# An encoder trunk on one core: the SSD scan rebuilt from log-decay tiles, loops written out, one convolution tap moved to ScalarE

## The chip, the cores and the metric

One core of a Trainium2 chip runs the whole program. The metric is the device time of one execution in microseconds (us), lower is better. TensorE (PE) multiplies matrices into eight PSUM banks, VectorE (DVE) and ScalarE (ACT) work elementwise, GpSimd (POOL) makes constants and issues some DMAs, SyncE (SP) issues the weight loads. Semaphores written by hand order the engines.

## What is computed

Two requests of 256 tokens (512 together) pass two layers of: half-step SwiGLU, a mixing stage, half-step SwiGLU. The mixing stage adds a convolution branch and a two-way state-space scan (SSD), each behind a gate. The scan, cut to what matters (one direction; `q` is a chunk of 128 tokens, so a request has two chunks):

```
    a = dtc * A ;  a_cum = jnp.cumsum(a, axis=2) ;  xdt = xc * dtc[..., None]
    seg = a_cum[:, :, :, None] - a_cum[:, :, None, :]
    decay = jnp.exp(jnp.where(tril, seg, -jnp.inf))
    scores = jnp.einsum("bcign,bcjgn->bcijg", Cc, Bc)
    y_diag = jnp.einsum("bcijgr,bcjgrp->bcigrp", scores[..., None] * decay, xdt)
    states = jnp.einsum("bcjgn,bcjgrp->bcgrpn", Bc, xdt * exp(a_cum[:, :, -1:] - a_cum))
    ... states carried from chunk to chunk ...
    y_off = jnp.einsum("bcign,bcgrpn->bcigrp", Cc, prev) * jnp.exp(a_cum)[..., None]
    y = y_fwd + y_bwd + xs * D_skip
```

x, B and C come out of a 5-tap convolution over tokens and a SiLU; the convolution branch has 31 taps.

## The kernel before

All activations stand as tiles of 128 features by 512 tokens. A **slab** is a 128x1024 block of weights: SP loads it into one of four slots (`wraw`), ACT rounds it to `whi` (L445), DVE makes the remainder `wlo` (L765), and PE multiplies eight pieces of it, three matmuls of 512 columns each (24 in all, L1139). ACT and DVE split a slab three slabs ahead of PE.

The mixing stage of a layer goes over eight groups of four heads, and two rounds more for gates. A group is eight steps `t` = 0 to 7, and in each step every engine does its share in program order: PE multiplies one slab (the projections gate, a, B, C, x, x, z, z of group `g`) and puts a piece of the SSD of group `g-1` behind it; DVE does four steps of the 5-tap convolution of `g`, some of the 31 taps of group `g-1` (`unit_tap`, L928, cut over the steps by `TAP_SLICES`), and its part of the SSD. So each layer has eight SSD groups, 16 in the program.

The SSD of a group, before, on PE: at t=0 transposes of x (L1297) and of B (L1303), and the scores of each chunk (L1307, 128x128 fp32); at t=1 the norm's sum (L1313) and, at t=1 and t=2, `seg` for four chunks in two directions: a product with `rtm` (L1249), the mask `never` (L1251) and four narrow products, one for each head (L1254); at t=3 the states (L1330), at t=4 their use for the other chunk (L1337); at t=4 and t=5 the product of weights and x with 64 moving columns for each chunk and head (`y_chunks`, L1264), and at t=5 and t=6 the transposes of that result (L1274). ACT takes the exponentials (`exp_seg`, L593), copies x, B, scores and states out of PSUM. DVE adds the two directions and multiplies by the scores (`decays`, L956, L961), scales x (L999), adds the states' part (L1014, L980), and gates. GpSimd sends the gated branch `tg` to DRAM (`v_spill`) and back into a padded tile (`vp`). Ahead of group 0, `dt_steps` makes the step sizes and sums of log decays, and DVE zeroes the pads (L1060, L1061).

Layers, groups 2 to 7 of a layer, and the feed-forward parts are hardware loops (`Fori`), with register arithmetic for semaphore values and addresses.

Of the kernel before, what the change touches and what calls it, by code (L numbers as in the profile page):

```python
# [5 lines left out]
F32 = mybir.dt.float32  # L28
F32R = mybir.dt.float32r
# [13 lines left out]
def trunk(nc, io):  # L43
# [47 lines left out]
    ND, NA = 16, 6  # L91
    NB = NC // 2

    v_dram = nc.dram_tensor("v_spill", [2, KD, P, SEQ], F32, kind="Internal").ap()
# [8 lines left out]
    with ExitStack() as ctx:  # L103
# [10 lines left out]
        selr = sb("selr", [P, 2, 2 * NH])  # L114
# [29 lines left out]
        with ExitStack() as s2:  # L144
            wd_raw = sb("wd_raw", [P, 8, P], at=s2)
            wd_hi = sb("wd_hi", [P, 8, P], F32R, at=s2)
            wd_lo = sb("wd_lo", [P, 8, P], F32R, at=s2)
            dx = sb("dx", [2 * NH, T], at=s2)
            de = sb("de", [2 * NH, T], at=s2)
            du = sb("du", [2 * NH, T], at=s2)  # L150
            dl = sb("dl", [2 * NH, T], at=s2)
            dc = sb("dc", [2 * NH, T], at=s2)
            dtf = sb("dtf", [2 * NH, 2, T], at=s2)
            aT = sb("aT", [P, NC, 2 * NH], at=s2)
            cumS = sb("cumS", [P, NC, 2 * NH], at=s2)
            ddS = sb("ddS", [P, NC, 2 * NH], at=s2)
        mix = sb("mix", [P, KD, T])
        with ExitStack() as s3:
            E = sb("E", [P, NC, 2, HPG * P], at=s3)
        ga = sb("ga", [P, KD, T])  # L160

        with ExitStack() as s3:
            tg = sb("tg", [P, T], at=s3)
            xpad = sb("xpad", [P, 2, 2, SEQ + TAPS - 1], at=s3)
# [3 lines left out]
            SC = sb("SC", [P, NC, P], at=s3)  # L168
            bT = sb("bT", [P, NC, P], at=s3)
            ytm = sb("ytm", [P, 2, GF], at=s3)  # L170
            dtT = sb("dtT", [P, NC, 2 * NH], at=s3)
            exT = sb("exT", [P, NC, 2 * NH], at=s3)
            wT = sb("wT", [P, NC, 2 * NH], at=s3)
# [5 lines left out]
        with ExitStack() as s3:  # L179
            yz = sb("yz", [P, 2, T], at=s3)  # L180
            rg = sb("rg", [P, T], at=s3)
        mtmp = sb("mtmp", [P, 2, T])
        mu = sb("mu", [P, T])
        with ExitStack() as s3:
            xw = sb("xw", [P, NC, GF], at=s3)
            zcur = sb("zcur", [P, 2, T], at=s3)
            yoff = sb("yoff", [P, NC, GF], at=s3)
            vp = sb("vp", [P, 2, SEQ + 2 * HALO], at=s3)
            cacc = sb("cacc", [P, 2, T], at=s3)
            rt = sb("rt", [P, NC, P], F32R, at=s3)  # L190
            rtm = sb("rtm", [P, NC, P], F32R, at=s3)
            exg = sb("exg", [P, NC, HPG], at=s3)
            wg = sb("wg", [P, NC, HPG], at=s3)
            selg = sb("selg", [P, 2, 2, HPG], F32R, at=s3)
            cwg = sb("cwg", [P, DWK], at=s3)
        with ExitStack() as s4:
# [23 lines left out]
        wd_in, wd_hi_ready, wd_lo_ready, dt_ps, dt_dve, dt_act, dtr_ps, dtr_ev, rt_ps, rt_hi, rtm_hi = (  # L220
            sem(n) for n in "wd_in wd_hi_ready wd_lo_ready dt_ps dt_dve dt_act dtr_ps dtr_ev rt_ps rt_hi rtm_hi".split())
        rt_ready, cum_ps, ex_ready, wT_ready = (
            sem(n) for n in "rt_ready cum_ps ex_ready wT_ready".split())
        tg_ready, v_ready, v_out, pad_zero, pad_ready, cv_ready = (
            sem(n) for n in "tg_ready v_ready v_out pad_zero pad_ready cv_ready".split())
        conv_tap, bc_ready, z_ready, zcopied, small_ready, xt_ps, bt_ps, sc_ps, xt_ready, bt_ready, sc_ready, xw_ready = (
            sem(n) for n in "conv_tap bc_ready z_ready zcopied small_ready xt_ps bt_ps sc_ps xt_ready bt_ready sc_ready xw_ready".split())
        st_ps, st_ready, yoff_ps, yoff_ready, seg_ps, e_ready, t_ready, m_ready, y_ps, y_ready, yt_ps, gate_mid, gated, xd_ready = (
            sem(n) for n in "st_ps st_ready yoff_ps yoff_ready seg_ps e_ready t_ready m_ready y_ps y_ready yt_ps gate_mid gated xd_ready".split())
        gsq, gsq_sum, gst_ps, gln, gr_ready, y2_ready, y_out = (  # L230
            sem(n) for n in "gsq gsq_sum gst_ps gln gr_ready y2_ready y_out".split())
        vp_in, cw_ready, unit_tap_done, unit_done, c_out = (
            sem(n) for n in "vp_in cw_ready unit_tap_done unit_done c_out".split())
# [12 lines left out]
        TAP_SLICES = [(0, 8), (8, 14), (14, 18), (18, 23), (23, 27), (27, 29), (29, DWK), (DWK, DWK)]  # L246
        f32 = lambda ap: ap.bitcast(F32)
        chunk = lambda c: slice(c * P, (c + 1) * P)

# [12 lines left out]
        def _(sp):  # L262
# [11 lines left out]
            def ffn(L, f, base):  # L274
                s = L * NSLAB + base
                for p0, n in PARTS:
                    with sp.Fori(0, n // 2) as i:
# [4 lines left out]
                    with sp.Fori(0, KD // 4) as i:  # L282
# [5 lines left out]
            def columns(L, base, w, col):  # L288

                with sp.Fori(0, KD // 4) as i:  # L290
# [4 lines left out]
            with sp.Fori(0, DEPTH) as L:  # L295
                ffn(L, 0, 0)
                with sp.Fori(0, NG) as g:
# [7 lines left out]
                with sp.Fori(0, KD // 2) as i:  # L305
# [18 lines left out]
        def _(pool):  # L324
            g_ = nc.gpsimd

            for free, n in ((lo_ready, RING), (slab_done, RING), (sq_added, 1), (ab_free, 2), (pad_ready, 2), (cv_ready, 2), (z_ready, 2),
                            (conv_tap, 1), (xt_ps, 1), (xw_ready, 1), (yoff_ps, 1), (yoff_ready, 1), (sc_ps, 1),
                            (seg_ps, 1), (e_ready, 1), (m_ready, 1), (y_ps, 1), (y_ready, 1), (gated, 1), (xd_ready, 1),
                            (gst_ps, 1), (y2_ready, 1), (unit_tap_done, 1), (unit_done, 1), (y_split, 4), (ya_mid, 2)):  # L330
# [4 lines left out]
            g_.memset(selr[:, :, :], 0.0).then_inc(const_made, 1)  # L335
# [8 lines left out]
            n = 3  # L344
            for sign in range(2):
                for half in range(2):
                    pool.wait_ge(const_fix, n)
                    pool.sem_inc(pool_passed, 1)
                    g_.affine_select(out=selr[:, sign, :], in_=selr[:, sign, :], compare_op=ALU.not_equal,
                                     fill=1.0 - 2 * sign, base=-half * 2 * NH, pattern=[[-1, 2 * NH]],  # L350
                                     channel_multiplier=1).then_inc(const_fix, 1)
                    n += 1
# [7 lines left out]
            def group(L, g, slabs, ssd, norm):  # L360

                G = L * NG + g
                H = G - 1
                if ssd:

                    pool.wait_ge(seg_ps, H * NC + 1)
                    pool.wait_ge(yoff_ready, H * NB + 1)
                    pool.wait_ge(xw_ready, H + 1)
                    pool.wait_ge(ex_ready, L + 1)
                    pool.wait_ge(wT_ready, L + 1)  # L370
                    pool.sem_inc(pool_passed, 1)
                    h0 = g * HPG - HPG
                    src = selr[:, :, :].rearrange("p s (d h) -> p s d h", d=2)[:, :, :, bass.ds(h0, HPG)]
                    g_.tensor_copy(selg[:, :, :, :], src).then_inc(small_ready, 1)

                    for c in range(2):
                        src = wT[:, c:NC:2, bass.ds(h0 + c * NH, HPG)]
                        g_.tensor_copy(wg[:, c:NC:2, :], src).then_inc(small_ready, 1)

                    src = exT[:, :, :].rearrange("p (b c) x -> p b (c x)", b=2)[:, :, NH:3 * NH]  # L380
                    src = src.rearrange("p b (c h) -> p b c h", c=2)[:, :, :, bass.ds(h0, HPG)]
                    g_.tensor_copy(exg[:, :, :].rearrange("p (b c) h -> p b c h", b=2), src).then_inc(small_ready, 1)

                    pool.wait_ge(v_out, G * 16 + 16)
                    pool.wait_ge(pad_zero, L * 2 + 2)
                    pool.wait_ge(unit_done, H + 1)
                    pool.sem_inc(pool_passed, 1)
                    pool.dma_start(vp[:, :, HALO:HALO + SEQ],
                                   v_dram[:, bass.ds(g - 1, 1)].rearrange("r o p t -> p (r o) t")).then_inc(vp_in, 16)
                if slabs:  # L390
                    pool.wait_ge(v_ready, G + 1)
                    pool.sem_inc(pool_passed, 1)
                    pool.dma_start(v_dram[:, bass.ds(g, 1)].rearrange("r o p t -> p (r o) t"),
                                   tg[:, :].rearrange("p (r t) -> p r t", r=2)).then_inc(v_out, 16)
                if norm:
                    pool.wait_ge(y2_ready, G * 2 - 1)
                    pool.sem_inc(pool_passed, 1)
                    pool.dma_start(y_dram[bass.ds(g * 2 - 4, 2)].rearrange("k p t -> p k t"),
                                   yz[:, :, :]).then_inc(y_out, 16)
                if ssd:  # L400
                    pool.wait_ge(unit_done, H + 2)
                    pool.sem_inc(pool_passed, 1)
                    pool.dma_start(c_dram[:, bass.ds(g - 1, 1)].rearrange("r o p t -> p (r o) t"),
                                   cacc[:, 0, :].rearrange("p (r t) -> p r t", r=2)).then_inc(c_out, 16)

            with pool.Fori(0, DEPTH) as L:
# [5 lines left out]
                group(L, 0, True, False, False)  # L412
# [1026 lines left out]
```

## Time and profile before

| what | value |
|---|---|
| time, median of 3 runs | 3090.6 us (3089.87 to 3091.07) |
| the profiled execution: time / span | 3091.98 / 3090.5 us |
| PE busy | 3014.7 us (98%) |
| DVE / ACT busy | 1909.0 (62%) / 1210.4 us (39%) |
| POOL busy | 88.8 us (3%) |

The span is what the profile covers. Matmuls are pipelined: the duration of one is its time in the pipeline, and the price of one is the distance from its start to the start of the next. A share of busy time is a mean over stages with different limits.

### The profile page before, as it was taken

The numbers are of one execution on the slowest core, as the hardware profiler recorded it, in microseconds if no ns is written. First come the engines' busy times: TensorE is split into PE (matmuls) and PEld (weight loads), VectorE is DVE, ScalarE is ACT, GpSimd is POOL, SyncE is SP. The second block draws the span as 40 slices with busy tenths as digits, with TensorE's granted clock in tenths as the row PEclk, the third lists the DMA queues.
The fourth block names the chain that finished last, engine by engine and source line by source line (L and its number), as shares of the span: only waits on it lengthen the run. The fifth ranks groups of instructions, "written<-read, shape, count | busy, mean of one in ns | idle before, by whom it ended". The sixth has DMA issues, their size and how long they took to land.

```text
span 3090.5 us, 41274 instructions
## 1 busy us (share of the span) xinstructions
PE 3014.7 (98%) x13916; PEld 2499.7 (81%) x13916; DVE 1909.0 (62%) x2503; ACT 1210.4 (39%) x1611; POOL 88.8 (3%) x186
## 2 busy tenths in 40 slices
PE   7999989999999999999999998999999999999998
PEld 5888868888887787888878887888888877878886
DVE  5444578999993555444544445799899735554444
ACT  4322344445543434222342224444554444252223
POOL 0000000000000000000000000000000010000000
PEclk9999999999999999999999999999999999999999
DMA  4333322323234433333333332332333353333332
GB/s 144 95 95 95 96 69 83 97 85 89 84 95 124 132 103 89 102 95 96 96 96 95 95 95 82 85 86 82 95 91 89 86 167 98 96 88 98 99 92 78
DMA packets 523803, 298.34 MB, mean 97 GB/s; under 512 B 10399, under 2 KB 514215, under 8 KB 523687
## 3 DMA queue, kind: packets, MB, share of 16 engines
q1 hardware_dynamic: 511888, 261.65, 29.6%
q0 software_dynamic: 10176, 34.63, 3.3%
q8 instruction: 68, 1.11, 0.1%
q10 hardware_dynamic: 1623, 0.55, 0.1%
q14 instruction: 48, 0.39, 0.0%
HBM read 277.92 MB, written 18.87 MB: 96 GB/s over the span
## 4 chain that ended last, share of the span: by engine, by line
PE 94%; DVE 2%; issue 1%; ACT 1%; DMA 1%; DVEq 0%; ACTq 0%; SPq 0%; POOLq 0%; POOL 0%
PE bank L1139 84%; PE bank L1264 2%; PE bank L1254 2%; PE bank L1249 1%; PE bank L1251 1%; PE bank L1337 1%; PE bank L1330 1%; DMA yraw<-y_spill 1%; PE bank L1307 0%; PE bank L1361 0%; PE bank L1297 0%; PE bank L1274 0%; PE bank L1313 0%; DVE bc L949 0%; DVE acc L776 0%
## 5 line engine op out<-in xcount | busy, mean ns | idle before, releaser
L1139 PE MATMUL bank<-uhi,whi 128*128 128x512 f32 x2944 | 1166.3, 396 | 29.6 <-DVE ulo L807 21.6
L1139 PE MATMUL bank<-uhi,wlo 128*128 128x512 f32 x2944 | 1150.6, 391 | 0.0
L1139 PE MATMUL bank<-ulo,whi 128*128 128x512 f32 x2944 | 1149.3, 390 | 0.0
L765 DVE TENSOR_TENSOR wlo<-wraw,whi 128x1024 fp32r<-128x1024 f32 x496 | 605.5, 1222 | 307.7 <-ACT whi L445 297.1
L445 ACT ACTIVATE whi<-wraw 128x1024 fp32r<-128x1024 f32 x496 | 521.1, 1053 | 433.2 <-PE bank L1139 433.0
L1139 PEld LDWEIGHTS bank<-uhi,whi 128*128 128x128 f32 x2944 | 555.4, 189 | 150.0 <-issue 28.4
L1139 PEld LDWEIGHTS bank<-uhi,wlo 128*128 128x128 f32 x2944 | 554.8, 188 | 118.0
L1139 PEld LDWEIGHTS bank<-ulo,whi 128*128 128x128 f32 x2944 | 555.6, 189 | 113.3 <-issue 1.4
L1139 PE MATMUL bank<-hhi,whi 128*128 128x512 f32 x960 | 377.1, 393 | 7.4 <-DVE hlo L1041 4.1
L1139 PE MATMUL bank<-hhi,wlo 128*128 128x512 f32 x960 | 374.2, 390 | 0.0
L1139 PE MATMUL bank<-hlo,whi 128*128 128x512 f32 x960 | 374.2, 390 | 0.0
L928 DVE SCALAR_TENSOR_TENSOR cacc<-vp,cwg,cacc 128x512 f32<-128x512 f32 x464 | 322.1, 743 | 0.0
L1139 PEld LDWEIGHTS bank<-hhi,whi 128*128 128x128 f32 x960 | 180.6, 188 | 49.5 <-DVE hlo L1041 6.3
L1139 PEld LDWEIGHTS bank<-hlo,whi 128*128 128x128 f32 x960 | 180.7, 188 | 38.1 <-issue 1.0
L1139 PEld LDWEIGHTS bank<-hhi,wlo 128*128 128x128 f32 x960 | 180.5, 188 | 37.8
L530 ACT ACTIVATE hhi<-fb 128x512 f32 x88 | 55.6, 632 | 395.2 <-DVE fb L835 395.2
L949 DVE SCALAR_TENSOR_TENSOR bc<-xpad,prm,bc 128x512 f32<-128x512 f32 x256 | 191.4, 747 | 17.6 <-DVE bc L946 3.7
L849 DVE SCALAR_TENSOR_TENSOR xf<-bank,xf 128x512 f32 x64 | 44.2, 691 | 197.4 <-PE bank L1139 197.4
L832 DVE TENSOR_TENSOR fb<-bank,rbc 128x512 f32<-128x512 f32 x88 | 60.8, 690 | 140.9 <-PE bank L1139 140.9
L527 ACT ACTIVATE fa<-fa 128x512 f32<-128x512 f32 x88 | 55.6, 632 | 234.1 <-DVE fa L829 234.1
L642 ACT ACTIVATE xpad<-bank 128x512 f32<-128x512 f32 x64 | 38.3, 598 | 256.1 <-DVE bc L949 151.6
L838 DVE TENSOR_TENSOR hlo<-fb,hhi 128x512 f32 x88 | 60.9, 692 | 82.2 <-ACT hhi L530 82.2
(199 smaller groups left out, 2144.8 us busy)
## 6 DMA issues: line engine op xcount, KB each, us to landing
wraw<-in_ffn_w_up SPq DMA_DIRECT2D x179, 512.0 KB, 3.7
wraw<-in_w_in SPq DMA_DIRECT2D x160, 512.0 KB, 3.8
wraw<-in_ffn_w_down SPq DMA_DIRECT2D x64, 512.0 KB, 3.7
wraw<-in_ssd_w_out SPq DMA_DIRECT2D x32, 512.0 KB, 3.8
wraw<-in_ffn_w_down SPq DMA_DIRECT2D x32, 384.0 KB, 3.3
y_spill<-yz POOLq DMA_DIRECT2D x16, 512.0 KB, 3.1
yraw<-y_spill POOLq DMA_DIRECT2D x32, 256.0 KB, 3.5
wraw<-in_conf_w_out SPq DMA_DIRECT2D x16, 512.0 KB, 4.3
```

What stands on the lines that cost most here:

```text
L445: a_.activation(whi[:, t % RING, :], wraw[:, t % RING, :], ACT.Copy).then_inc(hi_ready, 1)
L527: a_.activation(fa[:, j, :], fa[:, j, :], ACT.Silu).then_inc(silu_ready, 1)
L530: a_.activation(hhi[:, bass.ds(i * 2 + j, 1), :], fb[:, j:j + 1, :], ACT.Copy).then_inc(hhi_ready, 1)
L765: v_.tensor_tensor(wlo[:, t % RING, :], wraw[:, t % RING, :], f32(whi[:, t % RING, :]), ALU.subtract).then_inc(lo_ready, 1)
L832: v_.tensor_tensor(fb[:, j, :], bank[2 * j + 1][:, :], rbc[:, :], ALU.mult).then_inc(ab_free, 1)
L838: v_.tensor_tensor(hlo[:, m, :], fb[:, j:j + 1, :], f32(hhi[:, m, :]), ALU.subtract).then_inc(hlo_ready, 1)
L849: v_.scalar_tensor_tensor(out=xf[:, m, :], in0=bank[4 + q % 2][:, :].unsqueeze(1), scalar=0.5, in1=xf[:, m, :], op0=ALU.mult, op1=ALU.add) ...
L928: v_.scalar_tensor_tensor(out=dst, in0=src, scalar=cwg[:, k:k + 1], in1=dst, op0=ALU.mult, op1=ALU.add).then_inc(unit_tap_done, 1)
L949: ins = v_.scalar_tensor_tensor(out=dst, in0=src, scalar=w, in1=dst, op0=ALU.mult, op1=ALU.add)
L1139: ins = t_.matmul(out, a[:, slot, w], b[:, at + k, :], start=start and k == 0 and a is whi and b is hi, stop=stop and k == nk - 1 and a is ...
L1254: ins = t_.matmul(out[:, chunk(h)], selg[:, 0, d, h:h + 1].broadcast_to([P, P]), rt[:, c, :], start=False, stop=h == HPG - 1, skip_group_c ...
L1264: ins = t_.matmul(bank[4][:, f:f + HEAD], E[:, c, 0, chunk(h)], xT[:, c, h * HEAD:(h + 1) * HEAD], start=True, stop=True)
```

## The change

**SSD.** The log decay from token j to token i becomes one product: a tile `R` holds, for a head, the rows of the table `Q` of running sums that belong to it (ACT copies `Q` scaled by a column of the selector `selm`: eight copies for each request and group), and `Lr` (same chunk) or `LX` (other chunk) is the left side. PE adds the mask as before. Each request has, for each chunk, both directions on the diagonal and the one direction that reaches the other chunk. There are no states, no transposes of B and no transposes of y: the scores are made for all 256 tokens of a request, the 128x256 weights `M` of a chunk and head multiply x from the right, and y comes out with features on partitions, two heads in the two halves of a bank. **Loops** are all written out. **5-tap convolution:** ACT makes the middle tap with its bias from the bank, and DVE adds four. **Gated branch:** written by DVE straight into one of two padded tiles `vp`, without DRAM; the 31-tap result is put into the same tile, and the last sum comes at t=7 in place of t=6. The preparation of a layer sets constant parts of `Q`, `Lr` and `LX` to 1.

The core of the diff:

```diff
-                def seg(c):
-                    for d in range(2):
-                        t_.matmul(heads, rtm[:, c, :], selg[:, 1, d, :].unsqueeze(2).broadcast_to([P, HPG, P]), start=True, ...
-                        t_.matmul(heads, identr[:, :], never[:, d, :].unsqueeze(1).broadcast_to([P, HPG, P]), ...
-                        for h in range(HPG):
-                            ins = t_.matmul(out[:, chunk(h)], selg[:, 0, d, h:h + 1].broadcast_to([P, P]), rt[:, c, :], ...
+                def seg_diag(r):
+                    pe.wait_ge(rs_ready, H * 16 + r * 8 + 8)
+                    need(pe, m_added, H * 4 + r * 2)
+                    need(pe, e_ready, H * EPG + r * EPR)
+                    for c in range(2):
+                        for d in range(2):
+                            out = heads(2 + 4 * c + d)
+                            t_.matmul(out, Lr[:, d, 2 * r + c, :], R[:, d, c, :, :], start=True, stop=False)
+                            t_.matmul(out, identr[:, :], never[:, d, :].unsqueeze(1).broadcast_to([P, HPG, P]), ...
+                def seg_cross(r):
+                    for c in range(2):
+                        pe.wait_ge(e_ready, H * EPG + r * EPR + 2 * c + 1)
+                        t_.matmul(heads(2 + 4 * c), LX[:, 2 * r + c, :], R[:, c, 1 - c, :, :], start=True, stop=True).then_inc(seg_ps, 1)
+                def y_rows(r):
+                    pe.wait_ge(m_ready, H * 4 + r * 2 + 2)
+                    for j in range(2):
+                        for c in range(2):
+                            for half in range(2):
+                                h = 2 * j + half
+                                ins = t_.matmul(bank[4 + r][half * HEAD:(half + 1) * HEAD, j * SEQ:(j + 1) * SEQ],
+                                                xT[:, 2 * r + c, h * HEAD:(h + 1) * HEAD],
+                                                M[:, r, c, h, :, :].rearrange("p c i -> p (c i)"), start=c == 0, stop=c == 1)
...
+                def selected(r):
+                    need(act, seg_ps, H * EPG + r * EPR)
+                    for d in range(2):
+                        for h in range(HPG):
+                            head = (g - 1) * HPG + h
+                            a_.activation(R[:, d, :, h, :], f32(Q[:, d, 2 * r:2 * r + 2, :]), ACT.Copy,
+                                          scale=selm[:, head:head + 1]).then_inc(rs_ready, 1)
...
+                        a_.activation(bc[:, j, :], bank[t % 2][:, :], ACT.Identity, scale=prm[:, mid:mid + 1],
+                                      bias=prm[:, P_CB + col:P_CB + col + 1]).then_inc(mid_tap, 1)
...
+                def scored(r):
+                    dve.wait_ge(sc_ready, H * 2 + r + 1)
+                    for c in range(2):
+                        dve.wait_ge(m_added, H * 4 + r * 2 + c + 1)
+                        dve.wait_ge(e_ready, H * EPG + r * EPR + 5 + c)
+                        part = M[:, r, c, :, :, :].rearrange("p h c i -> p h (c i)")
+                        v_.tensor_tensor(part, part, SC[:, 2 * r + c, :].unsqueeze(1).broadcast_to([P, HPG, SEQ]), ALU.mult)...
...
+                v_.memset(f32(Q[2 * NH:P, :, :, :]), 1.0).then_inc(ones_set, 1)
+                v_.memset(f32(Lr[0:2 * NH, :, :, :]), 1.0).then_inc(ones_set, 1)
+                v_.memset(f32(LX[0:2 * NH, :, :]), 1.0).then_inc(ones_set, 1)
...
-            with dve.Fori(0, DEPTH) as L:
+            for L in range(DEPTH):
```

On PE, in one group of the loop, steps 2 to 4 of the SSD before (each `L1139` slab between them is left out; L1249, L1251 and L1254 are `seg`, L1330 and L1337 the states and their use, L1264 the product with x):

```order
L1249 MATMUL bank6<-selg,rtm 128x512
L1251 MATMUL bank6<-never,identr 128x512
L1254 MATMUL bank6<-rt,selg 128x128 x4
L1249 MATMUL bank7<-selg,rtm 128x512
L1251 MATMUL bank7<-never,identr 128x512
L1254 MATMUL bank7<-rt,selg 128x128 x4
...
L1330 MATMUL bank6<-xw,bT 128x256 x2
L1330 MATMUL bank7<-xw,bT 128x256 x2
...
L1337 MATMUL bank6<-xw,bc 128x256 x2
L1337 MATMUL bank7<-xw,bc 128x256 x2
L1264 MATMUL bank4<-xT,E 128x64 x4
```

On PE, the same steps now (L1193 is `seg_cross`, L1185 and L1186 `seg_diag` of the second request, L1202 `y_rows` of the first):

```order
L1193 MATMUL bank2<-R,LX 128x512
L1193 MATMUL bank6<-R,LX 128x512
...
L1185 MATMUL bank6<-R,Lr 128x512
L1186 MATMUL bank6<-never,identr 128x512
L1185 MATMUL bank7<-R,Lr 128x512
L1186 MATMUL bank7<-never,identr 128x512
...
L1193 MATMUL bank2<-R,LX 128x512
L1193 MATMUL bank6<-R,LX 128x512
L1202 MATMUL bank4<-M,xT 64x256 x8
```

The narrow products are gone, the states' two products too, and the product with x has 256 moving columns in place of 64 and fills 64 output partitions in place of 128.

On ACT, step 2 and the start of step 3 of a group now (L378 is the split of a slab, L605 the middle tap, L607 the copy for the other taps, L545 an exponential, L531 `selected` for the second request):

```order
L378 ACTIVATE whi<-wraw 128x1024
L605 ACTIVATE bc<-bank0,prm 128x512
L607 ACTIVATE xpad<-bank0 128x2x256
L545 ACTIVATE M<-bank2 128x4x128
L545 ACTIVATE M<-bank6 128x4x128
L531 ACTIVATE R<-Q,selm 128x2x128 x8
L378 ACTIVATE whi<-wraw 128x1024
L605 ACTIVATE bc<-bank1,prm 128x512
```

Before, that place had a split, the copy into `xpad`, four exponentials and a split; the middle tap and the eight copies into `R` are new, and PE's `seg_diag` of step 3 waits for the last of the eight.

## Rows read from the trace of the kernel before

**Rows 1.** The page: busy engines; the fetch of instructions (queue 8).

```profile
PE 3014.7 (98%) x13916; PEld 2499.7 (81%) x13916; DVE 1909.0 (62%) x2503; ACT 1210.4 (39%) x1611; POOL 88.8 (3%) x186
...
q8 instruction: 68, 1.11, 0.1%
```

**Rows 2.** Busy time by stretch: one mixing group (columns as printed).

```profile
core 0: us, PE busy (x) PEld busy (x) DVE busy (x) ACT busy (x) POOL busy (x), PEclk, DMA share, GB/s
690.86:752.75 61.89, 61.89 (x320) 52.56 (x320) 56.80 (x83) 29.81 (x45) 3.72 (x8) 1.00 0.30 89
```

**Rows 3.** The chain that ended last, one mixing group: start, length, what.

```profile
690.86 1.73 PE bank L1264 x16
692.59 5.54 PE bank L1139 x24
698.57 10.94 PE bank L1139 x48
711.71 5.47 PE bank L1139 x24
721.57 5.50 PE bank L1139 x24
730.59 5.53 PE bank L1139 x24
736.12 1.73 PE bank L1330 x8
737.85 5.47 PE bank L1139 x24
743.32 1.73 PE bank L1337 x8
```

**Rows 4.** PE in order of time, step 0 of that group: start, us, instruction.

```profile
709.34 1.03 PE L1297 MATMUL bank<-ident,bc 128*128 128x128 f32 x8
710.22 0.60 PE L1303 MATMUL bank<-ident,bc 128*128 128x128 f32 x4
710.65 1.06 PE L1307 MATMUL bank<-bc 128*128 128x128 f32 x8
711.47 0.47 PE L1139 MATMUL bank<-uhi,whi 128*128 128x512 f32 x1
```

**Rows 5.** PE in order of time, step 2 of that group.

```profile
726.91 0.38 PE L1249 MATMUL bank<-selg,rtm 128*128 128x512 f32 x1
727.12 0.40 PE L1251 MATMUL bank<-never,identr 128*128 128x512 f32 x1
727.36 0.56 PE L1254 MATMUL bank<-rt,selg 128*128 128x128 f32 x4
```

**Rows 6.** PE in order of time, group 0: a product with 64 output partitions.

```profile
432.05 1.94 PE L1229 MATMUL bank<-ul,aT 128*64 128x256 f32 x8
433.92 0.71 PE L1234 MATMUL bank<-aT,ul 128*128 128x128 f32 x4
```

**Rows 7.** PE's groups in that mixing group: busy, mean ns | idle.

```profile
L1330 PE MATMUL bank<-xw,bT 128*128 128x256 f32 x8 | 1.9, 379 | 0.0
```

**Rows 8.** DVE's groups in that mixing group.

```profile
L961 DVE TENSOR_TENSOR E<-E,SC 128x512 f32<-128x512 f32 x4 | 2.6, 684 | 0.0
L946 DVE TENSOR_SCALAR bc<-xpad,prm 128x512 f32<-128x512 f32 x4 | 2.2, 540 | 0.0
L999 DVE TENSOR_TENSOR xw<-xT,wg 128x1024 f32<-128x1024 f32 x1 | 1.2, 1219 | 0.0
L992 DVE SCALAR_TENSOR_TENSOR tg<-tg,bank 128x512 f32<-128x512 f32 x1 | 0.7, 687 | 2.3 <-PE bank L1139 2.3
```

**Rows 9.** ACT's groups in that mixing group.

```profile
L593 ACT ACTIVATE E<-bank 128x512 f32<-128x512 f32 x8 | 4.2, 596 | 1.8 <-PE bank L1254 1.8
L666 ACT ACTIVATE yz<-bc,dskip 128x512 f32<-128x512 f32 x2 | 1.3, 711 | 0.0
```

**Rows 10.** DVE in order of time, ahead of group 0 of the first layer.

```profile
411.33 0.54 DVE L1061 MEMSET vp<- 128x572 f32 x1
413.64 0.74 DVE L860 TENSOR_SCALAR dx<-bank,dtbA 64x512 f32<-64x512 f32 x1 [1.78 <-PE bank L1361]
```

**Rows 11.** PE in order of time, step 3 of group 0 of the first layer.

```profile
426.37 0.49 PE L1139 MATMUL bank<-uhi,whi 128*128 128x512 f32 x1 [0.67 <-DVE tg L992]
```

**Rows 12.** The chain at the end of the first layer.

```profile
1546.42 2.71 issue
```

More of the change, by code:

```diff
@@ L276, in ffn @@
                 for p0, n in PARTS:
-                    with sp.Fori(0, n // 2) as i:
+                    for i in range(0, n // 2):
                         for q in range(4):
@@ L281, in ffn @@
                     s = s + 2 * n
-                    with sp.Fori(0, KD // 4) as i:
+                    for i in range(0, KD // 4):
                         for q in range(4):
@@ L288, in columns @@
             def columns(L, base, w, col):
-                with sp.Fori(0, KD // 4) as i:
+                for i in range(0, KD // 4):
                     for q in range(4):
@@ L304, in _ @@
                 columns(L, S_GA, W_IN, C_GA)
-                with sp.Fori(0, KD // 2) as i:
+                for i in range(0, KD // 2):
                     for q in range(4):
@@ L343, in _ @@
                              pattern=[[-1, P]], channel_multiplier=1).then_inc(const_fix, 1)
[L344 to L352, printed above, removed]
+            for q in range(P // NH):
+                pool.wait_ge(const_fix, 3 + q)
+                pool.sem_inc(pool_passed, 1)
+                g_.affine_select(out=selm[:, :], in_=selm[:, :], compare_op=ALU.not_equal, fill=1.0, base=-q * NH,
+                                 pattern=[[-1, NH]], channel_multiplier=1).then_inc(const_fix, 1)
             pool.wait_ge(const_fix, 7)
@@ L358, in _, with group @@
                 g_.dma_start(stage_rows(row, KD, 0), io[name].rearrange("l (t p) -> t l p", p=P)).then_inc(free, 16)
-            def group(L, g, slabs, ssd, norm):
+            def group(L, g, ssd, norm):
                 G = L * NG + g
-                H = G - 1
-                if ssd:
[L366 to L370, printed above, removed]
-                    pool.sem_inc(pool_passed, 1)
[L372 to L404, printed above, removed]
@@ L408, in _ @@
+            for L in range(DEPTH):
                 pool.wait_ge(prm2_ready, 2 * DEPTH + 4)
@@ L675, in y_hi @@
                 a_.activation(dst, yraw[:, k % 4, :], ACT.Copy).then_inc(yhi_ready, 1)
-            with act.Fori(0, DEPTH) as L:
+            for L in range(DEPTH):
                 ffn(L, 0, 0)
@@ L1258, in y_chunks, with heads @@
[L1258 to L1275 removed]
+                def heads(b):
+                    return bank[b][:, :].rearrange("p (h i) -> p h i", h=HPG)
@@ L1292, in group @@
                     if t == 0 and ssd:
+                        pe.wait_ge(bc_ready, H * 4 + 2)
+                        need(pe, gated, H * NB)
+                        for r in range(2):
+                            for c in range(2):
+                                ins = t_.matmul(bank[4 + r][:, c * SEQ:(c + 1) * SEQ], bc[:, 0, chunk(2 * r + c)], bc[:, 1, request(r)],
+                                                start=True, stop=True)
+                            ins.then_inc(sc_ps, 1)
                         pe.wait_ge(bc_ready, H * 4 + 4)
-                        pe.wait_ge(e_ready, H * 2 * NC + 1)
+                        need(pe, e_ready, H * EPG)
+                        need(pe, m_added, H * 4)
                         for c in range(NC):
@@ L1366, in _ @@
                 ins.then_inc(slab_done, 1)
-                group(L, 0, True, False, False)
-                group(L, 1, True, True, False)
-                with pe.Fori(2, NG) as g:
-                    group(L, g, True, True, True)
+                for g in range(NG):
+                    group(L, g, True, g > 0, g > 1)
                 group(L, NG, False, True, True, gate=0)
```

451 lines of the change are left out of this document (191 added, 260 removed).

## The prediction

> **What bounds the kernel now.** I read the page first: PE is busy for 98% of the span, VectorE for 62%, ScalarE for 39% [rows 1]. A mean says nothing of a stage, so I cut the trace by stretches. In one mixing group, taken from one group's second y product to the next one's, PE is busy for all of 61.89 us, VectorE for 56.80, ScalarE for 29.81 [rows 2]; the granted clock is full. The groups from the second to the seventh repeat this to 0.01 us. So where the change works, a group costs what PE has to multiply, and VectorE has 5 us to spare, of which 2.3 are a wait for PE itself [rows 8]. The chain of waits says the same: it runs from slab to slab on PE, and what stands between two slabs is the SSD [rows 3]. The eight slabs are 43.98 us of the 61.89; the other 17.9 us are the norm's sum and the SSD. The question is what that becomes, and whether anything begins to keep PE waiting.
>
> **What PE loses, in each group.** All by starts, not by durations. Step 0: the transposes of B take 0.43 us (710.22 to 710.65) and the scores 0.82 (to 711.47) [rows 4]; both go, 1.25. `seg` at step 2 fills the gap from 727.07 to 730.59, 3.52; at step 1 the gap is 4.39, and the same 3.52 of it are `seg`, the rest is the norm's sum, which stays [rows 3]. Both go: 7.04. States and their use: 1.73 each, 3.46. The y product: 1.73 for a pair of chunks, twice, 3.46. The transposes of y: the gap from 698.13 to 698.57, 0.44, twice, 0.88 [rows 3]. Together 16.09 us.
>
> **What PE gains, in each group.** An fp32 product runs as two passes: the order lists four products L1330, the trace eight instructions [rows 7]. Scores: four products of 256 columns, eight passes at 1.73/8 = 0.216 [rows 3], 1.73 us. Log-decay tiles: eight products with `R`, eight masks and four for the other chunk, 20 of 512 columns in one pass. The mask's distance to the next start is 0.24, that of the product ahead of it 0.21 [rows 5], a slab's matmul 5.47/24 = 0.228 [rows 3]; I take 0.23, so 4.6 us (4.2 to 4.8). y: 16 products of 256 columns, 32 passes, which fill 64 output partitions. The nearest row is such a product ahead of group 0: eight passes in 1.87 us, 0.234 each with the edges around them, against 0.216 for 128 partitions [rows 6, 3]. 32 passes are 6.9 to 7.5 us; I take 7.0, since there are 16 in a row and the edge falls on them once. Sum 13.3 us (12.8 to 14.0), so a group is 2.76 us shorter (2.1 to 3.3), and 16 of them 44 us (33 to 53).
>
> The Trainium skill says in TensorEngine Tiling (Array Packing), Key Properties, that a change of tiling mode drains TensorE, which speaks against products with 64 output partitions. The trace agrees in part: 1.87 against 1.73 for eight passes is 0.14 us for going in and out [rows 6, 3]; with two visits in each of 16 groups the rule would be worth 4.5 us, and the 7.0 holds a part of it.
>
> **Whether PE is kept waiting.** VectorE: the first tap of four tiles goes (2.2 us), scaling x goes (1.2), four 512-wide operations with the states and y go (I price them like the 0.684 us of L961, 2.7), and four multiplications by the scores grow from 512 to 1024 columns (0.68 to the 1.22 of L999, plus 2.2) [rows 8]. 56.80 becomes about 52.9 us in a group of 59.1: no more loaded than before, and its 2.3 us wait for PE stays as cushion.
>
> ScalarE: 16 copies into `R`, four exponentials more, four middle taps, one score copy more, three copies fewer. Exponentials and taps read 512 columns from a bank, 0.6 us [rows 9]. A copy into `R` has 256 columns and a scale from a tile; the 512-column one with such a scale takes 0.71 [rows 9], half the length gives about 0.4 (0.3 to 0.71). 29.81 + 6.4 + 2.4 + 2.4 - 1.2 is about 40 of 59.1 us. The tight place is step 3: PE's second `seg_diag` waits for the last of eight copies. From the end of slab 2, PE has 0.46 us of products and a slab of 5.47, 5.9 us. In the same time ScalarE must do the middle tap, the copy to `xpad`, two exponentials (2.4 to 2.5 us) and the eight copies (3.2), 5.7 us. It just fits; I put no wait here. If it is late, what is queued behind it on PE is slab 4 and all that follows.
>
> The other new waits have more room. `seg_diag` of step 1 stands behind two slabs, and its copies behind one. The product y of a request waits for `scored`, which VectorE does a step earlier. The gated branch waits at step 1 for the DMA of the convolution result, which POOL issues when step 7 of the group before ends, a slab and a half earlier. The 32 DMAs of `v_spill` and `vp` go; PE has no wait on them now.
>
> **Ahead of group 0, for each layer.** Here PE does wait: slab 3 starts 0.67 us late, for the gated branch behind the step-size chain [rows 11]. That chain starts when VectorE has zeroed the pads and PE has sent the step sizes; VectorE then has 1.78 us idle [rows 10]. The change fills 572 + 1024 + 1024 + 512 = 3132 columns more. At 0.54 us for 572 that is 3.0 us, 1.2 past the idle time, and these land on PE. The table itself takes VectorE some four small subtractions more, later in the group; bounds nothing to 2.5 us. I take 2.5 in all (1.2 to 3.7), two layers 5 us.
>
> **Loops.** In a group PE has no gap for a loop's register work, so nothing is to be had there. At the end of the first layer the chain holds 2.71 us in which no engine's work is shown, just where VectorE branches back to the start of the layer's loop [rows 12]; this goes (0 to 3 us). The Trainium skill (Runtime: NRT & Kernel Launch, Instruction fetch mechanics) says that a taken branch to a target outside the current pages stalls on the fetch; the trace agrees with that one gap of 2.71. Straight code is fetched more, but the fetch now has 0.1% of the DMA engines [rows 1]: nothing.
>
> **Sum.** -44 + 5 - 2.7 is -42 us against the span of 3090.5. The profiled execution took 3091.98, 1.4 above the median of the three runs; I take the difference from the median: 3049.
>
> **Rivals.**
> 1. *The two halves of y run side by side.* Successive pairs of passes go to output partitions 0 to 63 and 64 to 127. If the second pass of one half runs with the first of the next, 16 passes take about nine places: 3.9 us for both requests in place of 7.0, a group of 56.0, 50 us more off: 3000. VectorE's 52.9 and the 2.8 us of its gaps that aren't a wait for PE end at 55.7, so it would just follow. For it: the halves alternate in the order. Against: no rows show two products at once; those with 64 output partitions all use the same half [rows 6]. The Trainium skill (TensorE: Matmul & The Clock Gate, Part 3) says that matmuls to different column groups run concurrently; no run here shows it so far. 28%.
> 2. *ScalarE's copies are late at step 3.* At 0.55 us each PE waits about 1 us in each group, 16 us: 3065; at 0.71, 2.2 us: 3084. For it: the place has 0.2 us to spare. Against: ScalarE issues the next before the last has ended, so durations overstate it. 10%.
> 3. *Slower: alternating halves break the pipeline.* If a pass can't start before the one ahead is out, it costs its 0.379 [rows 7]: 32 are 12.1 us, a group 2.4 longer, 38 us more, 3131. It decides from 0.30 us a pass upwards. For it: halves switch every two passes and no row has such a switch. Against: 0.234 with the edges [rows 6]. With milder forms that end above the old time, 7%.
> 4. *No change:* a pass at just about 0.30 or a wait of 2.6 us in each group, 5%.
>
> **Chances and range.** The forecast, PE alone and passes in a row, has 50%. Its own range is 3036 to 3067: 33 to 53 us of the groups, 2.4 to 7.4 ahead of group 0, 0 to 3 of the branch. With the first rival's 3000 and most of the second's, 2990 to 3074 holds about 8 in 10. Faster or slower by over 0.2% (6 us, about what a measurement here can tell from no change): 0.88 faster, 0.05 the same, 0.07 slower.
>
> **What would show it.** In the profile after: groups of 59.1 us; 32 y passes of a group starting 0.216 us apart (pairs with one start would be rival 1, 0.3 and more rival 3); 20 log-decay products 0.23 apart; no wait of PE for the copies into `R` at `seg_diag`; VectorE at 53 us a group; PE waiting 1 to 3 us more in group 0; no 2.7 us gap between the layers. The prediction is wrong if the passes of y are paired or broken, or if PE waits in the groups.

## The result and the profile after

The changed kernel takes 2992.4 us (median of four runs, 2991.7 to 2993.2) where the kernel before took 3090.8 beside it: ratio 0.968, 95% interval 0.9663 to 0.9697, 98 us less. The forecast was 3049. The time is nearest to that of the first rival, in which the two halves of y run side by side (3000).

The page of the profile after, its row of busy engines and the fetch of instructions, which answer to [rows 1]; the span is 2989.6 us (3090.5 before):

```profile
PE 2915.7 (98%) x13000; PEld 2367.6 (79%) x13000; DVE 1858.8 (62%) x2375; ACT 1356.4 (45%) x1961; POOL 50.8 (2%) x90
...
q8 instruction: 83, 1.36, 0.2%
```

One mixing group, from one group's first y visit to the next one's, answers to [rows 2], with the same columns:

```profile
604.43:660.26 55.83, 55.83 (x263) 44.48 (x262) 53.20 (x74) 39.13 (x66) 1.45 (x2) 1.00 0.31 90
```

PE is still busy in all of the group, at the full clock, and the group has become 6.06 us shorter, not 2.76. Sixteen groups make 97.0 us of the 100.9 by which the two spans differ. PE in order of time shows two of the pieces that were priced, the scores (463.68 to 465.41) and one y visit, which is the y product of one request (561.58 to 563.46); the columns are start, us, instruction:

```profile
463.68 1.89 PE L1226 MATMUL bank<-bc 128*128 128x256 f32 x8
465.41 1.04 PE L1234 MATMUL bank<-ident,bc 128*128 128x128 f32 x8
...
561.26 0.39 PE L1075 MATMUL bank<-uhi,wlo 128*128 128x512 f32 x1
561.58 1.95 PE L1202 MATMUL bank<-M,xT 128*64 128x256 f32 x16
563.46 0.50 PE L1075 MATMUL bank<-uhi,whi 128*128 128x512 f32 x1
563.79 0.40 PE L1075 MATMUL bank<-ulo,whi 128*128 128x512 f32 x1
```

The scores take the 1.73 us of the forecast. A y visit, 16 passes, takes 1.88 us; 16 passes one behind the other would be 16 x 0.216 = 3.46. The trace has their starts in eight pairs 0.216 us apart, with 0.007 us between the two of a pair.

The second `seg_diag`, where the prediction saw the tight place, PE and ScalarE in order of time:

```profile
652.21 0.40 PE L1075 MATMUL bank<-uhi,wlo 128*128 128x512 f32 x1
652.45 0.40 PE L1185 MATMUL bank<-R,Lr 128*128 128x512 f32 x1
652.68 0.40 PE L1186 MATMUL bank<-never,identr 128*128 128x512 f32 x1
...
654.31 0.40 PE L1075 MATMUL bank<-uhi,whi 128*128 128x512 f32 x1
```

```profile
648.86 3.31 ACT L531 ACTIVATE R<-Q,selm 128x256 fp32r<-128x256 f32 x8
652.05 1.06 ACT L378 ACTIVATE whi<-wraw 128x1024 fp32r<-128x1024 f32 x1
```

The eight products take 1.86 us, 0.23 each. The last copy is done at 648.86 + 3.31 = 652.17 and PE starts at 652.45, without a wait.

DVE's and ACT's groups in that mixing group, with the columns of [rows 8, 9]:

```profile
L531 ACT ACTIVATE R<-Q,selm 128x256 fp32r<-128x256 f32 x16 | 6.6, 506 | 0.0
L918 DVE TENSOR_TENSOR M<-M,SC 128x1024 f32<-128x1024 f32 x4 | 4.7, 1218 | 0.9 <-ACT M L545 0.9
L605 ACT ACTIVATE bc<-bank,prm 128x512 f32<-128x512 f32 x4 | 3.1, 780 | 11.8 <-DVE bc L901 10.0 <-PE bank L1075 1.7
L942 DVE SCALAR_TENSOR_TENSOR vp<-tg,bank 128x512 f32<-128x512 f32 x1 | 0.7, 689 | 1.4 <-PE bank L1075 1.4
```

Ahead of group 0 of the first layer, VectorE, then PE in group 0; these answer to [rows 10, 11]:

```profile
413.12 0.91 DVE L998 MEMSET Lr<- 64x1024 f32 x1 [0.27 <-issue]
414.09 0.48 DVE L999 MEMSET LX<- 64x512 f32 x1
414.50 0.62 DVE L814 TENSOR_SCALAR dx<-bank,dtbA 64x512 f32<-64x512 f32 x1
```

```profile
426.58 0.50 PE L1075 MATMUL bank<-uhi,whi 128*128 128x512 f32 x1 [1.21 <-DVE vp L942]
...
452.67 0.50 PE L1075 MATMUL bank<-uhi,whi 128*128 128x512 f32 x1 [1.69 <-ACT xpad L607]
```

VectorE's idle 1.78 us are gone, PE waits 1.21 in place of 0.67 at slab 3, and there is a new wait of 1.69 us at slab 7. Over the whole of group 0 a layer loses 1.3 us net.

One thing is not as the section on the change has it: the loops are not all written out. The loops over layers and groups are, with those of the weight loads; eight loops stay in the changed kernel, on ScalarE, VectorE and TensorE, in the feed-forward parts and in the stage behind the groups where the convolution branch's output is projected.

### The profile page after: what moved, and what is told of

Same layout as the page of the kernel before. It is cut to its first block and busy times, and to the rows that moved or that the text cites. A ratio compares the mean times of both kernels' runs of the same rounds, so it can differ in the third digit from the quotient of the medians.

```text
span 2989.6 us, 34559 instructions
## 1 busy us (share of the span) xinstructions
PE 2915.7 (98%) x13000; PEld 2367.6 (79%) x13000; DVE 1858.8 (62%) x2375; ACT 1356.4 (45%) x1961; POOL 50.8 (2%) x90
## 3 DMA queue, kind: packets, MB, share of 16 engines
q8 instruction: 83, 1.36, 0.2%
## 5 line engine op out<-in xcount | busy, mean ns | idle before, releaser
L378 ACT ACTIVATE whi<-wraw 128x1024 fp32r<-128x1024 f32 x496 | 521.6, 1054 | 433.2 <-PE bank L1075 422.9
L605 ACT ACTIVATE bc<-bank,prm 128x512 f32<-128x512 f32 x64 | 49.9, 779 | 194.4 <-DVE bc L901 158.3
```

The source lines that it names most:

```text
L378: a_.activation(whi[:, t % RING, :], wraw[:, t % RING, :], ACT.Copy).then_inc(hi_ready, 1)
L605: a_.activation(bc[:, j, :], bank[t % 2][:, :], ACT.Identity, scale=prm[:, mid:mid + 1], bias=prm[:, P_CB + col:P_CB + col + 1]).then_inc( ...
```

## The experiments

Theory: the gain beyond the forecast is y, whose two column halves share TensorE. Rivals: that it is the two passes of one fp32 product that run together; that the loops were worth more; and, of the other terms, that the places called tight had room.

**The order of the halves.** Two runs change only the order of the y passes. The first sets the halves wholly apart, the second changes them every four passes:

```diff
-                    for j in range(2):
-                        for c in range(2):
-                            for half in range(2):
+                    for half in range(2):
+                        for j in range(2):
+                            for c in range(2):
```

```diff
                     for j in range(2):
-                        for c in range(2):
-                            for half in range(2):
+                        for half in range(2):
+                            for c in range(2):
```

> The changed kernel with the y product of a request in another order: the eight passes for output partitions 0 to 63 first, then the eight for 64 to 127, where the changed kernel switches halves every two passes. Theory (a pass of one half runs beside a pass of the other, if they stand next to each other in the order): only the one place in the middle can be shared, so 16 passes take 15 places of 0.216 us and the edges, about 3.4 us in place of 1.88; 32 visits make +48 us, about 3041 us, and the passes start one by one, 0.216 us apart. Rival (it is the two passes of one product that run side by side): the order changes nothing, 2992 us, still eight pairs. Second rival (each half has a queue of its own that reaches far ahead): also 2992 us.

Measured: 3019.4 us, ratio to the kernel before 0.9768 (0.9752 to 0.9784), 27 us above the changed kernel.

> The changed kernel with halves switched every four passes in place of every two. Theory (neighbours in the order share a place): three switches, three shared places, 13 places of 0.216 us and the edges, about 2.95 us a visit, +34 us, about 3027 us. Rival (two passes of one product side by side): 2992 us. Second rival (queues of their own that reach at least four passes ahead): 2992 us as well, and then the run with the halves wholly apart says how far they reach.

Measured: 2992.8 us, ratio 0.9679 (0.9663 to 0.9695), no change from the changed kernel. Neither number is that of neighbours alone, and the first is not that of the two passes of one product. The second rival is left, in which a pass of one half can start ahead of passes of the other that stand before it in the order, and the first run says how far ahead. One y visit with the halves apart, PE in order of time, and PE in the first 0.26 and the first 0.92 us of it, counting y passes alone (the x behind the first busy time is their number):

```profile
564.35 2.86 PE L1202 MATMUL bank<-M,xT 128*64 128x256 f32 x16
567.14 0.50 PE L1075 MATMUL bank<-uhi,whi 128*128 128x512 f32 x1
```

```profile
564.34:564.60 0.26, 0.25 (x1) 0.19 (x2) 1.00 0.21 43
564.34:565.26 0.92, 0.91 (x4) 0.60 (x5) 1.00 0.76 223
```

The same stretch of a visit in the changed kernel:

```profile
561.57:561.83 0.26, 0.25 (x2) 0.20 (x4) 1.00 0.00 0
```

In the changed kernel two passes start at once; with the halves apart one does, and the first four are alone. The fifth pass starts at 565.263 in the trace and the next at 565.269. The trace does not name the half of a pass, but the first pass of each half in a visit lasts 0.43 us and the others 0.38, and the one at 565.269 is the second of the 0.43 us: it is the first of the second half, and three of the first half are still to come. So four places are shared and 12 are used: a visit of 2.79 us, 0.91 more than 1.88, which is 29 us over 32 visits, against 27 measured. The reach is four passes; whether the limit counts passes, products or weight loads is not shown. With halves by four it is just enough: all eight pairs are there, five of them 0.013 us apart and the last three 0.057 (0.007 in the changed kernel), and a visit takes 1.93 us. A pair made of the two passes of one product would stand one place apart in every order.

> The changed kernel with the two full-width products of the cross decay put between the two halves of the first request's y product (the second request's y is as before). Theory (a pass of the other half can start ahead of its turn, but not past a product that needs all 128 columns): in each of 16 groups eight passes that shared places get places of their own, 8 x 0.216 = 1.73 us, +28 us, about 3020 us; a visit is then 16 places. Rival (the reach of about four passes crosses full-width products too): two passes stand between, so at least two pairs are left, +21 us or less, 3013 us or below.

```diff
-                def y_rows(r):
+                def y_rows(r, halves=(0, 1)):
...
-                            for half in range(2):
+                            for half in halves:
...
-                        seg_cross(1)
...
-                        y_rows(0)
+                        y_rows(0, (0,))
+                        seg_cross(1)
+                        y_rows(0, (1,))
```

Measured: 3025.0 us, ratio 0.9787 (0.9772 to 0.9802), 34 us above the changed kernel on that chip (2991.3). PE in order of time at step 4, first in this run, then in the changed kernel:

```profile
609.75 0.39 PE L1075 MATMUL bank<-uhi,wlo 128*128 128x512 f32 x1
610.07 1.94 PE L1202 MATMUL bank<-M,xT 128*64 128x256 f32 x8
611.94 0.73 PE L1193 MATMUL bank<-R,LX 128*128 128x512 f32 x2
612.60 1.94 PE L1202 MATMUL bank<-M,xT 128*64 128x256 f32 x8
614.47 0.50 PE L1075 MATMUL bank<-uhi,whi 128*128 128x512 f32 x1
```

```profile
603.66 0.39 PE L1075 MATMUL bank<-uhi,wlo 128*128 128x512 f32 x1
603.89 0.61 PE L1193 MATMUL bank<-R,LX 128*128 128x512 f32 x2
604.43 1.95 PE L1202 MATMUL bank<-M,xT 128*64 128x256 f32 x16
606.31 0.50 PE L1075 MATMUL bank<-uhi,whi 128*128 128x512 f32 x1
```

No pass crosses the two full-width products. They bring their semaphore waits with them, and the second half has one of its own here, so the run does not tell whether the width or a wait stops it. Eight passes of one half take 1.87 us, to the hundredth those of group 0 before [rows 6], and as long as 16 that share. From the slab's last product to the next slab's first the step takes 4.72 us against 2.65: 2.07 more, 33 us in 16 groups. The expectation had only the 1.73 of the places; the other 0.34 us come with the second visit to 64 columns: 0.13 inside the visits, the rest at their edges, where a full-width product and a pass start 0.32 us apart and the first two products behind a visit 0.34, in place of 0.23.

**Loops alone.** The kernel before, with every loop written out:

```diff
-            with dve.Fori(0, DEPTH) as L:
+            for L in range(0, DEPTH):
```

> The kernel before with all its hardware loops written out, and nothing else of the change. Theory: the loops cost only the branch between the two layers (from one layer's statistics to the next's 368.08 us became 364.10 with the change), so 3 to 4 us less, about 3087 us; the period of a mixing group stays 61.89 us. Rival 1: the loops' register work slowed the groups too, 10 us and more less, and the SSD is worth that much less. Rival 2: nothing, or a loss by more instruction fetch, 3090 us or above.

Measured: 3082.3 us, ratio 0.9972 (0.9961 to 0.9982), 9 us less than before and more than the theory's 3 to 4. The group's period is 61.89 as before, so rival 1 falls. This run writes out also the eight loops that the changed kernel keeps, so the 9 us are not the change's own share. Most of the gain is at the border between the layers. PE there, kernel before, then loops written out:

```profile
1550.29 0.79 PE L1139 MATMUL bank<-uhi,whi 128*128 128x512 f32 x1 [5.29 <-DVE ulo L807]
```

```profile
1544.70 0.50 PE L1139 MATMUL bank<-uhi,whi 128*128 128x512 f32 x1 [2.04 <-DVE ulo L807]
```

And the granted clock (behind the busy times) in the 5 us after these starts, before and with the loops written out:

```profile
1550.00:1555.00 5.00, 4.71 (x11) 3.75 (x12) 5.00 (x9) 3.22 (x5) 0.00 (x0) 0.50 0.05 17
```

```profile
1544.40:1549.40 5.00, 4.70 (x20) 3.80 (x21) 5.00 (x9) 4.98 (x8) 0.46 (x1) 1.00 0.39 106
```

PE waits 3.25 us less, and its clock, which fell to the lower level (1.2 GHz, 0.50 in the row) with the 5.29 us without work, stayed at full; the second is worth 2.4 us more. The rest, 3 us by the medians and 5 by the spans of the two profiled executions (3090.5 and 3079.5), lies in pieces of 0.2 to 2 at the starts of other stages.

**ScalarE's copies.** The eight copies for the second request are made twice:

```diff
+                            if r and sem is rs_ready:
+                                act.wait_ge(again, H * 8 + d * HPG + h + 1)
...
+                        selected(1, again)
                         selected(1)
```

> The changed kernel with ScalarE's eight copies into R for the second request made twice (the first time with no use), 3.3 us more of ScalarE in step 2 of each group. Theory (the place is as tight as the prediction had it; the trace shows the last copy 0.35 us ahead of PE): PE waits about 2.9 us ahead of its second diagonal in each of 16 groups, less what later slack gives back, which is nothing where PE is the bound: +46 us, about 3038 us. Rival (ScalarE had more room than that, since it can fall behind in step 2 and PE has other work first): 2992 us to 3005 us.

Measured: 3054.8 us, ratio 0.9877 (0.986 to 0.9893), 62 us more. PE in order of time in two groups that follow the same wait:

```profile
489.70 0.80 PE L1188 MATMUL bank<-R,Lr 128*128 128x512 f32 x1 [2.81 <-ACT R L533]
490.29 0.63 PE L1189 MATMUL bank<-never,identr 128*128 128x512 f32 x1
...
670.92 0.50 PE L1188 MATMUL bank<-R,Lr 128*128 128x512 f32 x1 [2.81 <-ACT R L533]
671.25 0.39 PE L1189 MATMUL bank<-never,identr 128*128 128x512 f32 x1
```

The granted clock behind each:

```profile
489.69:494.50 4.81, 4.80 (x11) 3.80 (x12) 2.71 (x4) 4.55 (x8) 0.00 (x0) 0.50 0.26 67
...
670.90:674.50 3.60, 3.58 (x16) 2.95 (x17) 2.65 (x4) 3.60 (x7) 0.00 (x0) 1.00 0.04 9
```

The wait is the one expected, 2.8 us in nearly every group (43.8 us in all), and the place is as tight as the prediction had it. What the expectation lacked: with about every second of these waits the clock falls to half, and products start 0.43 us apart for 3 to 6 us. From then on periods of 58.93 and 60.52 us alternate for the most part, against 55.83, and the 62 us are these.

**What is next after PE.** Two runs: the middle tap back on VectorE, and the masks left out.

```diff
-                        a_.activation(bc[:, j, :], bank[t % 2][:, :], ACT.Identity, scale=prm[:, mid:mid + 1], ...
...
+                        ins = v_.tensor_scalar(dst, src, w, prm[:, P_CB + col:P_CB + col + 1], ALU.mult, ALU.add)
```

> The changed kernel with the middle tap of the 5-tap convolution given back to VectorE (five taps there, none on ScalarE). VectorE has 53.07 us of work in a group of 55.83 and waits 1.42 us of it for PE; four first taps are about 2.2 us more. Theory (what PE now saves takes nearly all of VectorE's room, so the tap's move is needed): VectorE runs over by 0 to 1 us a group, 0 to +16 us, about 3004 us (2992 to 3008), and PE begins to wait for VectorE in the groups. Rival (VectorE has room still, and the move of the tap was worth nothing): 2992 us, within 3.

Measured: 2996.5 us, ratio 0.9695 (0.968 to 0.971); the times alone do not tell it from the changed kernel's 0.968. The trace tells more: from the second on, groups take 56.23 to 56.33 us in place of 55.83, and PE waits for VectorE in them, at the norm's sum (five groups):

```profile
L1240 PE MATMUL bank<-sq,ones 128*128 128x512 f32 x10 | 5.6, 644 | 0.9 <-DVE sq L932 0.9
```

So without the tap's move VectorE would have made a group 0.4 to 0.5 us longer, in the lower half of the theory.

```diff
-                    a_.activation(dst, src[:, :].rearrange("p (h i) -> p h i", h=HPG), ACT.Exp).then_inc(e_ready, 1)
+                    a_.activation(dst, src[:, :].rearrange("p (h i) -> p h i", h=HPG), ACT.Exp, scale=0.0).then_inc(e_ready, 1)
...
-                            t_.matmul(out, Lr[:, d, 2 * r + c, :], R[:, d, c, :, :], start=True, stop=False)
-                            t_.matmul(out, identr[:, :], never[:, d, :].unsqueeze(1).broadcast_to([P, HPG, P]), ...
+                            t_.matmul(out, Lr[:, d, 2 * r + c, :], R[:, d, c, :, :], start=True, stop=True) ...
```

> The changed kernel without the eight mask products of a group; so that exponentials stay finite, ScalarE takes them with a scale of 0, which leaves out the decay and the causal mask. PE has 8 x 0.23 = 1.84 us less in each group of 55.83. Theory (PE is still what sets a group, and VectorE is next, 1.42 us behind it): 1.4 to 1.84 us a group less, -22 to -29 us, about 2968 us, with PE beginning to wait for VectorE. Rival (the change already ran into VectorE or ScalarE, and PE's 55.83 hide it): under 10 us less, 2983 us or above.

Measured: 2972.1 us, ratio 0.9615 (0.960 to 0.963), 20 us below the changed kernel, just short of the theory's 22 to 29. A group takes 54.75 us, and PE waits at the same place:

```profile
599.00:653.75 54.75, 54.30 (x256) 42.89 (x255) 53.22 (x74) 39.25 (x66) 1.45 (x2) 1.00 0.32 92
```

Of the 1.84 us that PE loses, 1.08 come off the time. VectorE is next, 1.1 us behind PE and not 1.42. Its work is the same 53.2 us; it waits about 1.5 us a group for ScalarE's exponentials (7.4 us in five groups), 0.9 of which it waited in the changed kernel too, so ScalarE likely belongs to the chain that is next.

**The preparation of a layer.** The fills go to GpSimd, and the last step of the table comes behind the taps:

```diff
+                g_.memset(f32(Q[2 * NH:P, :, :, :]), 1.0).then_inc(ones_set, 1)
...
-                    if slabs and not ssd:
+                    if slabs and not ssd and t != 5:
                         dt_steps(L, t)
...
+                    if slabs and not ssd and t == 5:
+                        dt_steps(L, t)
...
-                v_.memset(f32(Q[2 * NH:P, :, :, :]), 1.0).then_inc(ones_set, 1)
...
```

> The changed kernel with the preparation of a layer relieved: the three fills with 1 are made by GpSimd instead of VectorE, and the last step of the step-size table on VectorE comes behind that step's convolution taps. Theory (what a layer lost ahead of and in group 0, 1.3 us net in the trace, is VectorE's added work in the chain that PE waits for): 1 to 3 us less a layer, 2987 to 2990 us, and PE's waits for VectorE and ScalarE in group 0 get shorter. Rival (GpSimd and VectorE get in each other's way, or the waits have other causes): 2992 us or a little above.

Measured: 2984.4 us, ratio 0.9654 (0.9641 to 0.9668), below the 2987 to 2990 of the theory. This and the changed kernel were then run once more, on one chip:

> The changed kernel unaltered, on the same chip as the next run, to have its time beside that run's: 2992 us.

> The kernel whose layer preparation is relieved (GpSimd makes the fills, the last step of the table comes behind the taps) once more, beside the changed kernel on one chip. If its traces are right (2.4 us and 2.7 us less in group 0 of the two layers, 1.6 us less at the border between the layers, where the clock did not fall), it is 6 us below the changed kernel, 2986 us; if the 8 us between the medians of two chips were the chips, it is within 2 us of it.

Measured: 2991.3 us (0.968, 0.9666 to 0.9693) and 2983.2 us (0.9652, 0.9639 to 0.9666). The second is 8 us below the first, more than either expectation had; by the spans of the two profiled executions (2987.0 and 2980.4) it is 6.6. Group 0 of it, VectorE and PE:

```profile
413.79 0.74 DVE L819 TENSOR_SCALAR dx<-bank,dtbA 64x512 f32<-64x512 f32 x1 [1.81 <-PE bank L1277]
```

```profile
426.37 0.50 PE L1079 MATMUL bank<-uhi,whi 128*128 128x512 f32 x1 [0.67 <-DVE vp L947]
```

The step-size chain waits for PE again as before, PE's wait at slab 3 is the 0.67 of [rows 11], and the one at slab 7 is gone: 2.5 and 2.8 us less in the two layers. The gain at the border of the layers did not come again, since that was the clock of the changed kernel: after the same 2.04 us of waiting it fell in the first profiled execution and stayed at full in the second. The rows around the border, first and second (the granted clock stands behind the busy times):

```profile
1500.00:1505.00 5.00, 5.00 (x16) 3.90 (x15) 5.00 (x9) 4.52 (x7) 0.00 (x0) 0.66 0.40 105
```

```profile
1497.00:1503.00 6.00, 3.96 (x18) 2.88 (x17) 5.21 (x9) 5.15 (x9) 0.88 (x1) 1.00 0.63 175
```

Two more waits of 2.04 us, at 1136 and 2607, differ in the same way; each of the three falls costs 1.5 to 1.6 us. Differences of a few us between two single executions are thus no sign of a change.

## Why the prediction was wrong

**The step that failed** is the price of the y product: "32 passes are 6.9 to 7.5 us; I take 7.0". It measured 2 x 1.88 = 3.76. The row it rests on [rows 6] is right for what it shows, and the run with full-width products between the halves gives the same 1.87 us for eight passes; but in that row all passes go to one half, and so it could not show what happens between two halves. The price of a pass was right, the count of places was not: 16 in place of 32. With 3.76 the sum of that part becomes 16.09 - (1.73 + 4.6 + 3.76) = 6.0 us a group, and 6.06 was measured. Rival 1 had the mechanism and, with nine places for the measured eight, 3.9 us; that 2992 lies inside the wide range (2990 to 3074) is owed to this rival and not to the sum. The sentence of the Trainium skill that stood beside it (TensorE: Matmul & The Clock Gate, Part 3: matmuls to different column groups run concurrently) agrees with the eight pairs of starts. What the runs here add is that a pass can start four passes ahead of its turn, and that none did so across two full-width products.

**What held.** PE remains what sets a group, at 55.83 of 55.83 us. The scores 1.73 us, the log-decay products 0.23 each. VectorE 53.2 us a group (52.9 forecast), ScalarE 39.1 (about 40). A copy into `R` is 0.41 from start to start (0.4), though its duration reads 0.506; the middle tap is 0.78, not 0.6. The place at step 3 has 0.28 us to spare (0.2), and the run with the copies made twice shows that PE pays for what is over. Rival 2 rested on durations, which overstate the copies, as the prediction said.

**Group 0**: 2.5 us a layer were forecast (1.2 to 3.7), 1.3 measured. The mechanism at slab 3 is the forecast's: VectorE's fills take 2.3 us and eat the idle 1.78. The table's work on VectorE showed up as the 1.69 us at slab 7. The prediction left out that PE's own part of the preparation gets shorter: from the product with 64 output partitions to slab 4 it was 2.66 us (432.05 to 434.71), and is 1.87 now. The run with the relieved preparation takes the added waits away and keeps this, so it ends below the kernel before in group 0. It makes both changes at once, so which of them ended which wait is read from the order of work on VectorE and not from runs of their own.

**Loops**: 2.7 us were forecast at the border (0 to 3). The border gave 4.0 in the first profiled execution of the changed kernel and 5.6 in the second; with every loop written out and nothing else it is 5.6 there and 9 in all. The gap of [rows 12] was read rightly as a wait that goes (3.25 us). What was missing is that the clock fell with the 5.29 us that PE waited there, and some small starts of stages.

**The sum, in the spans of the profiled executions**: 97.0 from the groups, 2.6 lost in group 0, 4.0 gained at the border, 2.5 at other starts: 100.9, against 98 in the medians. Why the other starts gained is open; with the loops alone they gained too.

## What to carry to other kernels

Price a product by the places that it takes in TensorE, not by its passes: two products that fill different halves of the columns shared a place here when they stood within four passes of each other and nothing of full width lay between. A row of the trace prices only the pattern that it shows; where the change has a new pattern (here alternating halves), that row's price is one end of a range, and a mechanism that makes it half as long is the other. A wait on the bound engine costs its length and sometimes the clock behind it: 2.8 us of waiting cost 3.1 us in one group and 4.7 in the next, and 3.25 us less of it gave 5.6.

## What the runs showed of the hardware that was not expected

- Passes of two column halves run side by side, and a pass starts up to four passes ahead of its turn: with the halves switched every two or every four passes, 16 passes take eight places of 0.216 us; with eight of one half first, 12. None crossed two full-width products that stood between, with their semaphore waits.
- A visit to 64 output columns costs more than its passes: 0.14 us inside (1.87 for eight passes against 1.73), whether the halves are shared or not, and 0.1 us on either side (561.26 to 561.58 and 563.46 to 563.79, where slab products start 0.23 us apart). Behind fp32 products of full width the last of these stands too (0.31 us, 466.20 to 466.51), so it need not come from the columns.
- With waits of 2.8 us in a stretch of full clock, TensorE ran at the lower level (0.50) behind some and at full behind others, mostly by turns; after 2.04 us at three places it differed between two executions of one kernel; with 5.29 us it fell.
- With every loop of the kernel before written out, the instructions that ran went from 41,274 to 34,596 and their fetch (queue 8) from 1.11 to 1.80 MB, the row below, and no group became longer. With the change, eight loops left, they are 34,559 and 1.36 MB.

```profile
q8 instruction: 110, 1.80, 0.3%
```
